# A 512-token hybrid layer on one core: a later start for GpSimd's weight split, sums that begin at the bias, one filler matmul less, and the last tile sent in four pieces

## What is computed

```python
mod = silu(c) @ w_ada + b_ada
shift, scale, gate = split(mod, 3)
h = rmsnorm(x, g_norm) * (1 + scale) + shift
q, k, v, z_attn, b_g, c_g, h_c, z_conv = split(h @ w_in)      # eight groups of 512 columns
y_attn = moba_attention(rope(q), rope(k), v)                  # 8 heads of 64
y_attn = rmsnorm(y_attn, g_attn_out) * silu(z_attn)
y_conv = b_g * causal_conv3(c_g * h_c)
y_conv = rmsnorm(y_conv, g_conv_out) * silu(z_conv)
x = x + gate * (concat(y_attn, y_conv) @ w_out)
return rmsnorm(x, g_final)
```

## Time and profile before

| | us |
|---|---|
| median of 3 runs | 283.23 (283.2 to 284.3) |
| the profiled execution | 284.16 |
| its span in the trace | 282.1 |
| TensorE busy | 267.4 (95%) |
| VectorE busy | 194.3 (69%) |
| ScalarE busy | 136.1 (48%) |
| GpSimd busy | 116.1 (41%) |

### The profile page before, as it was taken

The page is one execution under the profiler, slowest core; times in us unless marked ns, Lnnn a source line. Parts: engine busy times, 40 slices in busy tenths (PEclk is TensorE's granted clock), DMA queues, the critical chain, the costliest instruction groups (busy, mean ns, idle before and its releaser), DMA issues.

```text
span 282.1 us, 3726 instructions
## 1 busy us (share of the span) xinstructions
PE 267.4 (95%) x1308; PEld 219.4 (78%) x1308; DVE 194.3 (69%) x339; ACT 136.1 (48%) x227; POOL 116.1 (41%) x73
## 2 busy tenths in 40 slices
PE   5799999889999999999999999999999999999990
PEld 1577888668878888888888888888888888888880
DVE  3898888979989894959969685924573821305564
ACT  4846346347137545374344722646646674302332
POOL 2500000633706343056366323344754999922410
PEclk9999999979999999999999999999999999999997
DMA  5999953197812472209572122532922434500113
GB/s 203 380 422 417 407 190 110 64 417 229 240 61 74 111 188 77 74 6 342 203 195 84 69 75 76 151 74 74 294 81 74 159 138 173 201 2 0 74 74 150
DMA packets 11924, 45.38 MB, mean 161 GB/s; under 512 B 2049, under 2 KB 2049, under 8 KB 10498
## 3 DMA queue, kind: packets, MB, share of 16 engines
q1 hardware_dynamic: 11762, 44.89, 46.0%
q10 hardware_dynamic: 144, 0.26, 0.2%
HBM read 38.85 MB, written 2.10 MB: 145 GB/s over the span
## 4 chain that ended last, share of the span: by engine, by line
PE 89%; DVE 3%; issue 3%; DMA 2%; ACT 1%; SPq 1%; POOLq 0%; POOL 0%; DVEq 0%; ACTq 0%
PE ps L1009 21%; PE ps L1011 21%; PE ps L1010 21%; PE ps L1070 4%; PE ps L1155 3%; PE ps L1145 3%; PE ps L1133 3%; PE ps L1085 2%; DMA xt<-in_x 2%; PE ps L1091 2%; PE ps L1083 1%; PE ps L1089 1%; PE ps L1044 1%; DVE h_lo L732 1%; PE ps L1077 1%
## 5 line engine op out<-in xcount | busy, mean ns | idle before, releaser
L581 POOL TENSOR_TENSOR w_lo<-raw,w_hi 128x1024 fp32r<-128x1024 f32 x29 | 74.5, 2579 | 119.0 <-ACT w_hi L333 80.3
L1009 PE MATMUL ps<-h_lo,w_hi 128*128 128x512 f32 x200 | 79.2, 396 | 0.0
L1011 PE MATMUL ps<-h_hi,w_hi 128*128 128x512 f32 x200 | 78.0, 390 | 0.0
L1010 PE MATMUL ps<-h_hi,w_lo 128*128 128x512 f32 x200 | 78.0, 390 | 0.0
L1011 PEld LDWEIGHTS ps<-h_hi,w_hi 128*128 128x128 f32 x200 | 37.5, 188 | 8.0
L1009 PEld LDWEIGHTS ps<-h_lo,w_hi 128*128 128x128 f32 x200 | 37.6, 188 | 7.9
L1010 PEld LDWEIGHTS ps<-h_hi,w_lo 128*128 128x128 f32 x200 | 37.6, 188 | 7.4
L333 ACT ACTIVATE w_hi<-raw 128x1024 fp32r<-128x1024 f32 x29 | 30.2, 1052 | 6.0 <-DMA raw<-in_wslots 6.0
L692 DVE CUSTOM_DVE_ANT_0 mod_junk<-ada,c_bc 128x1024 f32<-128x1024 f32 x22 | 30.9, 1404 | 1.1
L399 ACT ACTIVATE probs<-probs,rmin 128x384 f32<-128x384 f32 (+3 forms) x32 | 17.5, 549 | 16.4 <-DVE rmin L817 16.4
L827 DVE TENSOR_SCALAR probs<-probs,prec 128x384 f32<-128x384 f32 (+3 forms) x32 | 19.8, 683 | 0.3
(11 more groups left out here) (147 smaller groups left out, 484.1 us busy)
## 6 DMA issues: line engine op xcount, KB each, us to landing
raw<-in_wslots SPq DMA_DIRECT2D x33, 512.0 KB, 3.3
ada<-in_ada SPq DMA_DIRECT2D x11, 1024.0 KB, 8.8
raw<-in_whead SPq DMA_DIRECT2D x8, 448.0 KB, 7.1
xt<-in_x SPq DMA_DIRECT2D x4, 512.0 KB, 5.0
qd<-qt SPq DMA_DIRECT2D x16, 128.0 KB, 2.4
kd<-kt SPq DMA_DIRECT2D x16, 128.0 KB, 2.4
x<-in_x SPq DMA_DIRECT2D x4, 512.0 KB, 6.7
out<-x SPq DMA_DIRECT2D x3, 512.0 KB, 2.7
```

The costliest lines, as they stand in the source:

```text
L581: nc.gpsimd.tensor_tensor(lo, src[:, :], hi.bitcast(F32), ALU.subtract).then_inc(s_lo, 1)
L1009: nc.tensor.matmul(o, a_hi, b_lo, start=start, stop=False)
L1010: nc.tensor.matmul(o, a_lo, b_hi, start=False, stop=False)
L1011: return nc.tensor.matmul(o, a_hi, b_hi, start=False, stop=stop)
```

## The change

There are four parts.

- Pool waits for the eighth `hlo_ok` (the last low part of h) before its first slot, and no longer for the sixteenth sum.
- The sum instructions take a first value, so that sh comes out of the shift sum itself with the bias in it, and the gate column out of the gate sums. The scale sum goes to `acc`, and ACT makes gs of it with a one-column Identity, in front of h_hi. The two small DVE instructions per chunk and the one for the gate column are gone. b1 now holds (bias + 1) * g_norm.
- One of the two `keep_warm(2 * P)` before the fourth x tile's transpose is gone.
- At the end, the last sum begins at the sum of the two other pieces plus EPS, so it writes what Pool reads. The last tile is scaled and sent in four pieces of 256 columns, two on ACT and two on DVE and SP.

```diff
-                act.wait_ge(mod_ok, 2 * j + 2)
+                act.wait_ge(mod_step, 2 * j + 1)
+
+                nc.scalar.activation(gs[:, j:j + 1], acc[:, j:j + 1], ACT.Identity, scale=prm[:, C_GN + j:C_GN + j + 1],
+                                     bias=b1[:, j:j + 1]).then_inc(mod_ok, 1)
+                act.wait_ge(mod_ok, j + 1)
+                act.wait_ge(mod_step, 2 * j + 2)
...
-            scale_left(TT - 1)
             m = TT - 1
-            act.wait_ge(fin_left, TT)
-            nc.scalar.dma_start(out[m * P:(m + 1) * P, 0:BANK], x2[:, m, 0:BANK]).then_inc(out_left, 16)
+            act.wait_ge(fin_rs, m + 1)
+            act.wait_ge(x2_left, 1)
+            for lo in (0, 2 * P):
+                nc.scalar.activation(x2[:, m, lo:lo + 2 * P], x2[:, m, lo:lo + 2 * P], ACT.Copy, scale=fin[:, m:m + 1]
+                                     ).then_inc(fin_left, 1)
+            for i, lo in enumerate((0, 2 * P)):
+                act.wait_ge(fin_left, TT + i)
+                nc.scalar.dma_start(out[m * P:(m + 1) * P, lo:lo + 2 * P], x2[:, m, lo:lo + 2 * P]).then_inc(out_left, 16)
...
-            pool.wait_ge(mod_step, 2 * KT)
+            pool.wait_ge(hlo_ok, KT)
             for n in range(12):
                 slot(n)
...
-            nc.vector.tensor_scalar(b1[:, :], prm[:, C_B + KT:C_B + 2 * KT], 1.0, None, ALU.add).then_inc(b1_ok, 1)
+            nc.vector.scalar_tensor_tensor(out=b1[:, :], in0=prm[:, C_B + KT:C_B + 2 * KT], scalar=1.0,
+                                           in1=prm[:, C_GN:C_GN + KT], op0=ALU.add, op1=ALU.mult).then_inc(b1_ok, 1)
...
-                dve.tensor_tensor_reduce(mod_junk[:, :], src[:, two, :], c_rows, 1.0, 0.0, ALU.mult, ALU.add,
-                                         acc[:, j, two:two + 1]).then_inc(mod_step, 1)
...
+                if j < KT and two == 0:
+                    to, first = acc[:, j:j + 1], 0.0
+                elif j < KT:
+                    to, first = sh[:, j:j + 1], prm[:, C_B + j:C_B + j + 1]
                 else:
...
+                    at = 2 * (j - KT) + two
+                    to, first = gcol[:, at:at + 1], prm[:, C_B + 2 * KT + at:C_B + 2 * KT + at + 1]
+                dve.tensor_tensor_reduce(mod_junk[:, :], src[:, two, :], c_rows, 1.0, first, ALU.mult, ALU.add,
+                                         to).then_inc(mod_step, 1)
...
+            dve.wait_ge(part_ok, 1)
             dve.wait_ge(x2_ok, len(PIECES))
-            dve.tensor_tensor_reduce(om[:, 1, 0:hi - lo], x2[:, m, lo:hi], x2[:, m, lo:hi], 1.0 / D, 0.0, ALU.mult, ALU.add,
-                                     ss2[:, 8:9]).then_inc(last_sq, 1)
-            sum_out(TT - 1)
-            scale_right(TT - 1)
+            dve.tensor_tensor_reduce(om[:, 1, 0:hi - lo], x2[:, m, lo:hi], x2[:, m, lo:hi], 1.0 / D, ss2[:, 12:13], ALU.mult,
+                                     ALU.add, fin_e[:, m:m + 1]).then_inc(fin_sum, 1)
+            dve.wait_ge(fin_rs, TT)
+            for lo in (BANK, BANK + 2 * P):
+                nc.vector.scalar_tensor_tensor(out=x2[:, m, lo:lo + 2 * P], in0=x2[:, m, lo:lo + 2 * P], scalar=fin[:, m:m + 1],
+                                               in1=gfin[:, lo:lo + 2 * P], op0=ALU.mult, op1=ALU.mult).then_inc(fin_right, 1)
...
                         else:
-                            keep_warm(2 * P)
                             keep_warm(2 * P)
                             pe.wait_ge(x_norm3, 1)
```

More of the change, by code:

```diff
@@ L147, in build @@
         gs, sh, b1 = sb("gs", [KT]), sb("sh", [KT]), sb("b1", [KT])
-        acc = sb("acc", [NADA, 2])
+        acc = sb("acc", [KT])
         gcol = sb("gcol", [KT])
@@ L193, in build @@
         y_norm, y_hi, y_lo = sem("y_norm"), sem("y_hi"), sem("y_lo")
-        gcol_ok, gate_out, gate_in = sem("gcol_ok"), sem("gate_out"), sem("gate_in")
+        gate_out, gate_in = sem("gate_out"), sem("gate_in")
         acc_out, om_ok, x2_ok, x2_sq, x2_g = sem("acc_out"), sem("om_ok"), sem("x2_ok"), sem("x2_sq"), sem("x2_g")
-        last_sq, x2_left = sem("last_sq"), sem("x2_left")
+        part_ok, x2_left = sem("part_ok"), sem("x2_left")
         fin_sum, fin_rs, fin_left, fin_right = sem("fin_sum"), sem("fin_rs"), sem("fin_left"), sem("fin_right")
@@ L281, in _ @@
                 if n == 20:
-                    sp.wait_ge(gcol_ok, 1)
+                    sp.wait_ge(mod_step, 2 * NADA)
                     sp.dma_start(gate_d, gcol[:, :]).then_inc(gate_out, 16)
@@ L296, in _ @@
             m = TT - 1
[L297 to L300, removed]
+            for i, lo in enumerate((BANK, BANK + 2 * P)):
+                sp.wait_ge(fin_right, TT + i)
+                sp.dma_start(out[m * P:(m + 1) * P, lo:lo + 2 * P], x2[:, m, lo:lo + 2 * P]).then_inc(out_done, 16)
+            sp.wait_ge(out_done, 16 * (TT + 1))
+            sp.wait_ge(out_left, 32)
         @block.scalar
@@ L541, in scale_left @@
                 act.wait_ge(fin_rs, m + 1)
[L542 to L545, removed]
+                act.wait_ge(x2_g, m + 1)
                 nc.scalar.activation(x2[:, m, 0:BANK], x2[:, m, 0:BANK], ACT.Copy,
@@ L691, in mod_half @@
                 c_rows = c_bc[:, :] if j else ps[:, 4 * BANK:6 * BANK]
-                dve.tensor_tensor_reduce(mod_junk[:, :], src[:, two, :], c_rows, 1.0, 0.0, ALU.mult, ALU.add,
-                                         acc[:, j, two:two + 1]).then_inc(mod_step, 1)
[L695 to L699, removed]
-                else:
-                    nc.vector.tensor_scalar(sh[:, j:j + 1], acc[:, j, 1:2], prm[:, C_B + j:C_B + j + 1], None,
-                                            ALU.add).then_inc(mod_ok, 1)
+                if j < KT and two == 0:
+                    to, first = acc[:, j:j + 1], 0.0
+                elif j < KT:
+                    to, first = sh[:, j:j + 1], prm[:, C_B + j:C_B + j + 1]
+                else:
+                    at = 2 * (j - KT) + two
+                    to, first = gcol[:, at:at + 1], prm[:, C_B + 2 * KT + at:C_B + 2 * KT + at + 1]
+                dve.tensor_tensor_reduce(mod_junk[:, :], src[:, two, :], c_rows, 1.0, first, ALU.mult, ALU.add,
+                                         to).then_inc(mod_step, 1)
             def scale_x(m):
@@ L711, in _ @@
             mod_half(0, 0)
-            mod_column(0, 0)
             mod_half(0, 1)
-            mod_column(0, 1)
             src, arrived, count = raw_place(0)
@@ L724, in _ @@
                         mod_half(j, two)
-                    for two in range(2):
-                        mod_column(j, two)
                 dve.wait_ge(hw_hi if j else hw_hi0, j if j else 1)
@@ L909, in _ @@
             mod_half(11, 1)
-            dve.wait_ge(mod_step, 2 * NADA)
-            nc.vector.tensor_tensor(gcol[:, :], acc[:, KT:, :].rearrange("p a b -> p (a b)"),
-                                    prm[:, C_B + 2 * KT:C_B + 3 * KT], ALU.add).then_inc(gcol_ok, 1)
             least(2, 0)
@@ L967, in sum_out @@
                 dve.wait_ge(x2_sq, e + 2)
[L968 to L976, removed]
+                nc.vector.tensor_scalar(fin_e[:, m:m + 1], ss2[:, e:e + 1], ss2[:, e + 1:e + 2], EPS,
+                                        ALU.add, ALU.add).then_inc(fin_sum, 1)
             def scale_right(m):
@@ L987, in _ @@
                     dve.wait_ge(x2_sq, 8)
-                    nc.vector.tensor_scalar(ss2[:, 12:13], ss2[:, 6:7], ss2[:, 7:8], None, ALU.add).then_inc(gcol_ok, 1)
+                    nc.vector.tensor_scalar(ss2[:, 12:13], ss2[:, 6:7], ss2[:, 7:8], EPS, ALU.add, ALU.add).then_inc(part_ok, 1)
                 residual(e)
```

## The result

| | median us | runs | against the kernel before, with 95% interval |
|---|---|---|---|
| before, beside it | 283.76 (283.2 to 285.04) | 4 | |
| changed | 279.63 (279.37 to 279.82) | 4 | 0.9842 (0.9801 to 0.9882) |

The change is 4.1 us faster by the medians. The four runs of the kernel before lie in two pairs (283.2 and 283.23, 284.3 and 285.04), and its median lies between them. The profiled execution took 279.57 us with a span of 277.5, where that of before took 284.16 with 282.1: 4.59 and 4.6 us less.

The account below looks back on a forecast made before the run. TensorE was taken as the bound, nine tenths of the chain that ended last. Terms 4.02 + 0.43 + 0.5 = 4.95 us gave 279.2 from the profiled 284.16, 278.3 from the median 283.23; range 277.4 to 280.8.

Parts of the forecast that it names:

- the gap: TensorE's wait for the last h_lo before chunk 7's low-part matmuls, around 55 us: 2.62 us, all expected to go.
- The collision: Head chunk 7: DVE's w_lo and h_lo each held for one Pool instruction; Pool's later first slot removes both holds.
- the 4.02 us: Gain at head chunk 7 from Pool's new wait: 2.62 us of idle TensorE plus 1.40 of low clock.
- The clock: Chunk 7's 14 low-part matmuls run at granted clock 0.50, taking 4.59 us for 3.19: 1.40 us to be regained.
- the end: After the last matmul: shorter last sum 0.31 us, last tile in four pieces 0.2; gain 0.5 us.
- the start: Chunks 0 and 1: sums beginning at the bias and one filler less give 0.12 + 0.31 = 0.43 us.
- Rival (b): TensorE's clock falls even so, with one filler gone: price 1.4 us, time 279.7; chance 0.06.
- (a): DVE follows too late for K1 because Pool's slots hold it in the rope and conv: say 280.2 us; chance 0.11.
- rival (d): Slower: Pool's slots hold DVE in rope and conv so often that K1 starts later: 286.6 us; chance 0.04.
- The middle: After 62.14 us the 4.45 us gain lasts; rq likely held, K1 keeps 1.2 us slack; cost 0, bounds 0 and 1.2.

Follow-up runs that it names:

- repeated recordings: The kernel before, unchanged, recorded three more times: 283.01, 284.56 and 283.07 us.
- late-Pool kernel: The changed kernel with Pool's first slot waiting for the fourth finished bank of the head, 4.1 us later: 281.16 us, ratio 0.9888.

## Why the prediction was right, point by point

**What bounds the kernel, and the gap: right.** The collision read in the earlier trace rows is gone, and with it the 2.62 us. TensorE's first low-part matmul starts at 54.57 instead of 57.55. One row was misread: the 0.2 us wait for h_hi is that of chunk 0, at 16.22. Chunk 1 has no row; its first matmul merely starts 0.49 us behind the one before it, where 0.23 is usual.

**That this part of the gain is the new wait's: wrong in its reason.** The prediction gave the 4.02 us to the wait, and let the earlier sums do no more than let DVE lead. It did work out that lead (h_lo at 52.1; it ended at 52.33), but did not ask what the lead does to the collision if the wait were not there. The kernel with the old wait shows it. w_lo starts 0.16 us ahead of Pool, and h_lo's hold ends 1.0 us before TensorE needs it. Either edit is enough, and the 4.02 came out although the reason given for it was only one of two.

**The clock: right in this recording, wrong as a constant.** In the recordings, 14 matmuls took 4.65 us up to H0's start before and 3.17 after: 1.48, predicted 1.40. Of this 0.1 belongs to any start behind the gap, since the repeated recordings with full clock have 3.29 and 3.27; the one with the low clock has 4.88. But the low clock comes only in some executions of the kernel before. The recorded one had it, and the 283.23 of the median hardly can have had it: each of the 25 runs with the lower mean clock took 284.0 or more. The step that failed is the last of the sum, "from the median the sum gives 278.3". It took 1.40 us off a median that did not contain them. The first form of the sum, 279.2 from the recorded 284.16, is 0.4 from the recorded 279.57. The measured 279.63 is 1.3 above the forecast of 278.3. Of that, 0.35 is the end and 0.07 the start (both below), and the other 0.9 is this base. Without the 1.40 the sum from the median is 279.7. Rival (b) asked whether the clock falls after the change; it should have asked how often it had fallen before.

**The range: partly luck.** The forecast's own span was 277.5 to 279.1, with 0.72 of the chances, and 279.63 lies outside it. It lies at the 279.7 of rival (b), which did not happen: there is no low clock near 57 us. The range held the time because it had been drawn wide enough for rivals (a) and (b). Faster by more than 1.4 us was right. In rival (d), four holds make 286.5 and not 286.6.

**The start: 0.36 for 0.43.** Chunk 1's first matmul starts at 21.46, for 21.82 in the earlier trace rows, although ACT squared the third x tile 0.3 us later in the second recording (8.72 for 8.43). The timeline after:

```profile
14.57 0.38 ACT L353 ACTIVATE gs<-acc,b,prm 128x1 f32<-128x1 f32 x1
...
19.12 1.28 DVE L709 CUSTOM_DVE_ANT_0 mod_junk<-ada,c_bc,prm 128x1024 f32<-128x1024 f32 x1
...
20.33 0.08 DVE L709 DVE_READ_ACCUMULATOR2_ANT sh<- 128x1 f32 x1
...
20.50 0.78 ACT L360 ACTIVATE h_hi<-ps,sh,gs 128x512 fp32r<-128x512 f32 x1 [1.10 <-DVE sh L709]
```

Two sizes were off. The one-column Identity takes 0.38 to 0.39 us, as much as the 128-column Copy that was the upper bound, and not 0.3. A sum that begins at a column takes 1.28 us, where one that begins at a constant takes 1.22. The filler alone gives nothing, as predicted. From the start of that square to chunk 1's first matmul it is 13.1 to 13.7 us in the seven recordings with the old start, 13.2 with the sums only, 13.6 with one filler less only, and 12.7 to 13.1 in the five recordings that have both. So the two together give about 0.5 (means 13.4 and 12.9), a little more than the 0.43. What the sums give alone can't be told from one recording. The times are no clearer: the kernel with the old wait and the one with only the sums ran on the same chip, and differ in the filler and the end; the first is 0.83 us faster by the medians. The end is 0.15 of that, and the traces show 0.2 for the filler (13.2 against 13.0). The rest is within the 0.7 over which the four runs of each spread.

**The middle: right.** rq was held once (2.72 us), the rope of Q0 came out 1.9 us earlier, y_conv 1 ended at 75.27, and K1 started at 76.27: 1.0 us of slack for the 1.2 worked out. The 4.46 us at H0 (62.20 to 57.74) are 4.45 at the last tile.

**The end: 0.15 for 0.5.** From the end of the last matmul to the end of the span it is 6.9 us, where 6.6 were predicted and 7.1 stood before. The shorter last sum gave 0.14 and not 0.31. The addition went, but the sum that takes its place in the chain starts 0.14 us behind the piece it squares (0.04 before) and takes 0.48 for 0.42. The four pieces gave 0. The second piece from SP starts at 274.44, 0.94 us behind the end of the power, where the single one started at 0.82; each half product takes 0.48 us. The 0.41 that was used for it is the row of another form, without the scalar. On ACT's queue, which ends last, the second piece starts 1.0 us behind the power, for 0.79. The landing is 2.1 us for 2.6 on SP and 2.4 for 2.8 on ACT (medians of two pieces; ACT's later one took 2.6), near the 2.4 of the row of 128 KB, so what is saved there pays for the later issue and the second instruction. By the page DMA: Bandwidth & Descriptors of the Trainium skill (Anatomy of one DMA) the difference of the landing would be 0.3 (an estimate from its fit for DMAs issued from GpSimd). Measured on SP and ACT it is 0.5 and 0.4, and the two kernels with four and two pieces differ by 0.1 us.

## What to carry to other kernels

When two edits touch the same collision, work out each of them without the other: here either was enough, and the gap would have gone with one. In a collision between two engines ask which instruction starts first; 0.3 us changed the order. Before a cost that one recording shows is taken off a median, see whether the median contains it: a spread of the runs that is wider than usual, their mean clocks, or recordings at both ends of the spread tell. And a one-column instruction that was folded into its neighbour gave back 0.14 us here and not 0.31, since the neighbour grew and started later.

## What the runs showed of the hardware

- The same 2.4 us of idle TensorE is followed by the low clock (0.50, 1.2 GHz, for about 3 us) in some executions and by full clock in others: three of six recordings each, 284.3 and 283.0 us on average, and by their mean clock 25 and 18 of 43 further runs, 284.7 and 283.3. With 1.46 us of fillers in the same wait and 1.0 us idle, the recording had full clock and none of ten runs was over 283.9. Behind the 1.2 us wait of the late-Pool kernel the one recording shows 1.00.
- The hold between DVE and Pool works in both directions and for the smallest instruction: Pool's power on one column took 0.93 us for 0.54 beside a DVE product with two SBUF inputs, which itself took its usual 0.69. The Trainium skill's page SBUF — State Buffer (Who interferes with whom) calls the shared ports an exclusive lock and says that the order of issue decides who blocks; the traces agree in both orders (DVE held: 2.83, 2.72 and 2.05 us for 0.69).
- An Identity of ACT on one column, with a column each as scale and bias, takes 0.38 to 0.39 us, as long as a Copy of 128 columns with a scale column only the earlier trace rows. The forms differ, so this does not show what the width costs.
